# Feed-forward stages of a two-block transformer kernel: every other weight tile begins with the products with the weights' rest

## The reference

```python
def swiglu(h, w_gate, w_up, w_down):
    return (jax.nn.silu(h @ w_gate) * (h @ w_up)) @ w_down
```

```python
x = x + 0.5 * swiglu(rms_norm(x, ffn1_norm), ...)        # gu0, down0
x = x + concat(fourier, attention) @ w_out
x = x + 0.5 * swiglu(rms_norm(x, ffn2_norm), ...)        # gu1, down1
x = x + short_conv_mixer(...); x = x + mem_cross_attention(...)
x = x + swiglu_2(rms_norm_2(x, norm_ffn[0]), ...)        # gu2, down2
x = x + moba_attention(...);   x = x + mem_cross_attention(...)
x = x + swiglu_2(rms_norm_2(x, norm_ffn[1]), ...)        # gu3, down3
```

## Time and profile before

| what | value |
|---|---|
| median of 3 runs | 1240.12 us (1239.66 to 1240.19) |
| span of the profiled execution | 1237.7 us |
| mean granted clock of PE | 0.999 |
| PE busy | 1229.1 us (99%), 7432 matmuls |
| PEld busy | 1095.2 us (88%) |
| DVE busy | 928.1 us (75%) |
| ACT busy | 658.7 us (53%) |
| POOL busy | 31.1 us (3%) |
| DMA | 221.74 MB, mean 179 GB/s |
| L418, all (2716 in the feed-forward stages and those that share the helper) | 416.3 + 246.1 us |
| L1271 (DVE, rest of a weight tile) | x202, 2299 ns |
| L916 (ACT, rounding of a weight tile) | x202, 1911 ns |

### The profile page before, as it was taken

The page is one execution under the profiler, slowest core; times in us unless marked ns, Lnnn a source line. Parts: engine busy times, 40 slices in busy tenths (PEclk is TensorE's granted clock), DMA queues, the critical chain, the costliest instruction groups (busy, mean ns, idle before and its releaser), DMA issues.

```text
span 1237.7 us, 18082 instructions
## 1 busy us (share of the span) xinstructions
PE 1229.1 (99%) x7432; PEld 1095.2 (88%) x7432; DVE 928.1 (75%) x1292; ACT 658.7 (53%) x872; POOL 31.1 (3%) x23
## 2 busy tenths in 40 slices
PE   9999999999999999999999999999999999999998
PEld 8888889978888888888888888889998888888887
DVE  7887866878777858988568777669968657877744
ACT  6655544456555444546546555445555445555632
POOL 0000000000000000440000000000000000000000
PEclk9999999999999999999999999999999999999999
DMA  9565664235555663556346555644445533555560
GB/s 329 187 213 177 224 209 164 75 137 172 187 186 188 214 216 131 186 188 211 130 138 233 188 190 186 222 170 152 156 142 182 187 136 137 204 200 177 198 209 34
DMA packets 51426, 221.74 MB, mean 179 GB/s; under 512 B 4464, under 2 KB 5776, under 8 KB 30864
## 3 DMA queue, kind: packets, MB, share of 16 engines
q1 hardware_dynamic: 51056, 220.25, 51.7%
q10 hardware_dynamic: 288, 0.33, 0.1%
HBM read 219.52 MB, written 1.05 MB: 178 GB/s over the span
## 4 chain that ended last, share of the span: by engine, by line
PE 92%; DVE 5%; issue 1%; DMA 1%; ACT 0%; SPq 0%; DVEq 0%; ACTq 0%
PE bank L418 48%; PE bank L462 21%; PE bank L422 7%; PE bank L449 5%; PE bank L507 2%; DVE wt L1271 2%; PE bank L761 2%; PE bank L789 2%; PE bank L484 1%; PE bank L510 1%; PE bank L489 1%; DMA raw<-weights 1%; PE bank L777 0%; PE bank L544 0%; DVE xn L1280 0%
## 5 line engine op out<-in xcount | busy, mean ns | idle before, releaser
L1271 DVE TENSOR_TENSOR wt<-raw,wt 128x2048 fp32r<-128x2048 f32 x202 | 464.1, 2299 | 67.8 <-ACT wt L916 67.4
L916 ACT ACTIVATE wt<-raw 128x2048 fp32r<-128x2048 f32 x202 | 386.0, 1911 | 119.7 <-PE bank L422 89.8
L418 PE MATMUL bank<-xn,wt 128*128 128x512 f32 x1712 | 416.3, 393 | 1.4 <-DVE scratch L1376 0.7
L418 PEld LDWEIGHTS bank<-xn,wt 128*128 128x128 f32 x1712 | 313.0, 188 | 63.0 <-DVE xn L1280 1.1
L418 PE MATMUL bank<-h,wt 128*128 128x512 f32 x1004 | 246.1, 392 | 0.0
L462 PEld LDWEIGHTS bank<-xn,wt 128*128 128x128 f32 x1824 | 234.3, 191 | 9.7 <-DVE wt L1271 0.8
L462 PE MATMUL bank<-xn,wt 128*128 128x256 f32 x1824 | 238.2, 283 | 0.2 <-DVE wt L1271 0.2
L418 PEld LDWEIGHTS bank<-h,wt 128*128 128x128 f32 x1004 | 182.5, 188 | 34.1 <-issue 0.4
L1376 DVE TENSOR_TENSOR scratch<-bank,rest 128x512 f32<-128x512 f32 x98 | 67.6, 690 | 86.9 <-ACT rest L928 86.8
L999 ACT ACTIVATE h<-scratch 128x256 fp32r<-128x256 f32 x88 | 36.8, 418 | 158.7 <-DVE scratch L1416 158.7
L928 ACT ACTIVATE rest<-bank 128x512 f32<-128x512 f32 x114 | 67.6, 593 | 65.9 <-PE bank L462 64.4
(11 more groups left out here) (227 smaller groups left out, 972.3 us busy)
## 6 DMA issues: line engine op xcount, KB each, us to landing
raw<-weights SPq DMA_DIRECT2D x158, 1024.0 KB, 4.9
raw<-weights SPq DMA_DIRECT2D x88, 512.0 KB, 4.9
raw<-weights SPq DMA_DIRECT2D x8, 256.0 KB, 4.5
k_t<-mem_t SPq DMA_DIRECT2D x2, 1024.0 KB, 8.1
raw<-weights SPq DMA_DIRECT2D x8, 128.0 KB, 4.1
out_t<-work SPq DMA_DIRECT2D x4, 256.0 KB, 2.3
x<-x_t SPq DMA_DIRECT2D x3, 256.0 KB, 5.3
v_s<-fourier SPq DMA_DIRECT2D x2, 256.0 KB, 5.3
```

The lines of the kernel that those rows point to most:

```text
L418: return pe.matmul(out, hi, a.rearrange("p a s -> p (a s)"), start=first, stop=False, skip_group_check=True)
L916: act.activation(wt[t % RING][:, 0], raw[t % RING][:], ACT.Copy).then_inc(weight_hi, 1)
L1271: dve.tensor_tensor(wt[t % RING][:, 1], raw[t % RING][:], wt[t % RING][:, 0].bitcast(F32), ALU.subtract).then_inc(weight_lo, 1)
```

## The change

A turned order for some tiles of the feed-forward stages: first the 16 products with the rest (waiting for `weight_lo` before the first), then the 16 with the rounded weights; in `square_tile` under `turned`, in `down` as `turned_run`. Turned are, in the gate/up stages, the odd tiles from 3 on (in gu0 from 15 on), and in each down stage the slots 1, 3, 6 and 8. The products are the same, their order within the tile is another. The first product of a turned gate/up tile opens the bank (`start`) with the upper half alone, and the products with the rounded weights write the lower half for the first time with `start=False`.

```diff
+                if turned:
+                    pe.wait_ge(weight_lo, t + 1)
+                    for k in range(*ks):
+                        for m in range(ms):
+                            pe.matmul(out[:, m, S:2 * S], w[:, 1, m * KB + k, :], a[:, k, 0, :], start=k == 0, stop=False,
+                                      skip_group_check=True)
+                    for k in range(*ks):
+                        if k in beside:
+                            beside[k]()
+                        for m in range(ms):
+                            mm = pe.matmul(out[:, m, :], w[:, 0, m * KB + k, :], a[:, k].rearrange("p a s -> p (a s)"), start=False,
+                                           stop=k == KB - 1, skip_group_check=True)
+                    mm.then_inc(tile_done, 1)
+                    return
...
+            def turned_tile(n, j):
+                return j % 2 == 1 and j >= (15 if n == 0 else 3)
+
...
+                def turned_run(i, rows, d):
+
+                    w = wt[(t0 + i) % RING]
+                    blocks = [(at + m, k, bank[:, 2 * PAIR[name, 2 * d + m // 2] + m % 2, :]) for at, k in rows for m in range(4)]
+                    pe.wait_ge(weight_lo, t0 + i + 1)
+                    for at, k, out in blocks:
+                        with_rest(out, w[:, 1, at, :], h[:, k], False)
+                    for at, k, out in blocks:
+                        mm = with_hi(out, w[:, 0, at, :], h[:, k], False)
+                    return mm
...
-                    if i < FF // 4:
+                    if i in (1, 3):
+                        mm = turned_run(i, rows_at(0, range(4 * i, 4 * i + 4)), 0)
+                    elif i < FF // 4:
                         mm = run(i, rows_at(0, range(4 * i, 4 * i + 4)), 0, range(4), True)
...
+                    elif i in (6, 8):
+                        mm = turned_run(i, rows_at(0, range(4 * i - FF, 4 * i - FF + 4)), 1)
```

More of the change, by code:

```diff
@@ L422, in with_rest, with square_tile @@
                 return pe.matmul(out[:, S:2 * S], lo, a[:, 0, :], start=False, stop=last, skip_group_check=True)
-            def square_tile(t, out, a, ready=None, beside={}, lows=None, ks=(0, KB), ms=2, cuts=(), narrow=False, late=None):
+            def square_tile(t, out, a, ready=None, beside={}, lows=None, ks=(0, KB), ms=2, cuts=(), narrow=False, late=None, turned=False):
                 w = wt[t % RING]
+                if turned:
[12 more added lines that the diff above has]
+                    return
                 for k0, k1 in zip((ks[0], *cuts), (*cuts, ks[1])):
@@ L601, in gate_up @@
                                 cuts=((2, 4, 6) if j == 0 else (4,)) if in_parts else (4, 6) if j == 0 else (),
-                                late=KP * OPERAND[name] if j == 0 and n else None)
+                                    late=KP * OPERAND[name] if j == 0 and n else None, turned=turned_tile(n, j))
             def down(n_ffn, norm_name, beside={}):
```

## The result

| what | before | changed |
|---|---|---|
| median | 1239.73 us (1239.60 to 1240.19, 5 runs) | 1245.18 us (1245.12 to 1245.38, 5 runs) |
| ratio | | 1.0045, 95% interval 1.0033 to 1.0056 |
| span of the profiled execution | 1237.7 us | 1243.6 us |
| mean granted clock | 0.999 | 0.998 |

The changed kernel is 5.45 us slower. The forecast said slower, by 3.5 us, with a range from 1241.8 to 1245.3, which is 1.7 to 5.2 us above the median of 1240.12 that it stood on. The direction and the five places were right; the size was 2 us short and lies above that range. This is half again as much as forecast, so a term of the sum is missing or too small.

The account below looks back on a forecast made before the run. PE's instruction stream was taken as the bound. Profiled 1237.7 - 1.0 (switches) + 4.5 (late rests) = 1241.2 us; on the median, 1240.12 + 3.5 = 1243.7 us, range 1241.8 to 1245.3.

Parts of the forecast that it names:

- the five places: Tile 5 of gu1, gu2, gu3 and slot 1 of down0, down1: PE waits for late rests, 4.53 us in sum.
- PE's stream is the time, and a wait is lost whole: Whole run: PE is busy 99%, only 1.1 us of waits from 137 us on, so any new wait lengthens it equally.
- The delay is given back: Rival: a DVE that has caught up removes PE's later 1.1 us of waits on DVE or ACT, 1242.6 us; chance 0.11.
- Switches, 0.020 us for each turned tile: At 50 turned tiles, one pair of size switches saved each: 1.0 us gained, bounds 0 and 1.5.
- The switch saves nothing: Rival: turned tiles gain nothing from saved switches and the five waits stay, 1244.7 us; chance 0.13.
- the other side: Rival: a pair of switches is worth more than 0.02 us at every turned tile; at 0.11, 1239.1 us; chance 0.06.
- Which tiles are late: Of 50 turned tiles, 45 have at least 1.09 us to spare; five get DVE's rest 0.12 to 1.90 us late.
- Lateness + 0.15: Cost of a late rest: lateness plus 0.05 us to hear of it and 0.10 to get going; down1 2.05.
- Why they are late: Slot 1 of down0, down1: half tile 21 brings PE early, its quarter pieces queue ahead of L1271; 1.52, 1.90 late.
- The clock: Rival: PE's clock falls in the two long waits of down0 and down1, 1248.7 us; chance 0.06.
- The price of a fall: A fall behind a down wait costs 2.5 us, taken from the start-up's L798 products, which ran slow for 5.0 us.
- by it the two waits would cost about 5 us more: Down0 and down1 slot 1: by the skill's section, PE's waits can lower the clock, about 5 us for both.

Follow-up runs that it names:

- the next run: The changed kernel with 6 products of ones with ones in both waits, ahead of slot 1 of down0 and of down1: 1243.89 us.

## Why the prediction was right and where it was wrong

- **PE's stream is the time, and a wait is lost whole:** right. What was lost at down0 is still there 1100 us later; the rival "The delay is given back" falls. In the trace with the longer wait the whole addition stays to the end as well.
- **Switches, 0.020 us for each turned tile:** right, term and sign. Pairs take 0.02 less, and 45 of them measured 0.83 us against 0.9. That interval just touches no gain; the traces, in which every pair starts 0.02 us further ahead than the one before, decide it. The rival "The switch saves nothing" falls, and so does the other side.
- **Which tiles are late:** all five, and no sixth, with the lateness read from L1271's end against the tile's start. Tile 5 of gu1 to gu3 cost 0.34 to 0.39 each against 0.27 to 0.33, down0's slot 1 1.65 against 1.57. "Lateness + 0.15" was 0.02 to 0.12 too low at these places and at down1's slot 1 without the clock's part (2.10 against 2.05). The two parts of the 0.15 were also off, in opposite directions: the products start 0.15 us after L1303's end, where the earlier trace rows had 0.05, and the stretch behind the wait takes 0.07 to 0.08 us more than 1.91, not 0.10.
- **Why they are late (DVE's queue behind the half tile):** right; moving one step on DVE removed both waits and 5.2 us.
- **The clock:** here it failed. The step is "by the rows seen, nothing; no row decides for this length", after which the sum took the fall at nothing, and its chance was put at 0.06. What the runs showed in its place: one fall behind one of the two waits, worth 3.65 - 2.10 = 1.55 us at down1, or 3.15 - 1.65 = 1.5 us at down0 in the run with the wait of down1 filled (read at the start of slot 3; the expectation of the next run has 2.99). The longest wait that was weighed was 0.69 us; the new ones are more than twice as long, and silence of the trace was taken for an answer.
- **The price of a fall** was also wrong, in the other direction: 2.5 us by the start-up's slow stretch, which lasted 5 us. The one behind down1's wait lasted from 423.99 to 427.41, and half of that, 1.7 us, is the most that it could cost. Two falls were priced together, as if both or none came; every trace seen has one fall behind a wait, or none.
- **How near the repaired sum comes.** With one fall the forecast's own terms give 1243.7 + 1.55 = 1245.25, against 1245.18 measured. Part of this agreement is luck, since the forecast stood on 1240.12 and the kernel before measured 1239.73 beside the changed one: as a difference it is 5.1 against 5.45 us. The two profiled spans, 5.9 us apart, leave 0.8 us open, which the table above places: 0.26 in the start-up, 0.3 for waits a little dearer than forecast, 0.25 of the switches' gain that didn't come. The medians show less than half of it. Without the clock's part the difference is 4.00 us with both waits filled, against 3.5.
- **The rule that was weighed.** The section of the Trainium skill that was weighed (TensorE: Matmul & The Clock Gate, "HAM oscillation — how this bites in real kernels") pointed the right way: the trace agrees with it that waits of PE between groups of products can bring the clock down, here in the windows at 0.50 to 0.75. But the waits in that section's own case are longer than the two here, so "by it the two waits would cost about 5 us more" went beyond what it says.

The trace before did hold a sign, outside the rows used: at the end of the run, where PE has stopped. First its last row in the timeline, then the window over the end:

```profile
1232.03 0.38 PE L563 MATMUL bank<-con,col_x 128*128 128x128 f32 x2
1229.00:1237.00 8.00, 3.41 (x30) 3.17 (x29) 3.59 (x10) 2.21 (x6) 0.00 (x0) 0.86 0.35 131
```

PE's last product ends at 1232.41, and the mean clock of the window is 0.86: it is 1.00 up to 1234, 0.87 in the next microsecond and 0.50 from 1235 on. So the clock fell 2.3 us after PE stopped. That is no proof for a wait of 1.9 us, but it is nearer to it than 0.69. The page's slices of 31 us print a 9 over this fall as over a full clock.

What stays open is what makes the clock fall behind a given wait in one execution and not in the next. The four traces with a fall behind a wait (of 1.56, 1.88, 1.90 and 1.90 us) say this much: it came 0.4 to 0.7 us after PE had resumed, not in the wait. The five runs of the changed kernel all lie within 0.3 us, so each seems to have had one fall, though only one was profiled in detail.

## What to carry to other kernels

Before an engine's order is turned so that it asks for an operand earlier, lay the end of the operand's producer beside the new first use, for every instance and not for the steady state: 45 tiles had over a microsecond to spare here, and five decided the sign. Where the bound is PE, count a new wait of one to two microseconds with the clock behind it, some 1.5 us more, as a case with a real chance. A fall of some microseconds doesn't show in the page's slices; ask for the granted clock in narrow windows. And the same two tiles made PE wait for nothing once the producer's queue, not the consumer's, was reordered.

## What the runs showed of the hardware

- Behind a wait of PE of 1.56 us its clock fell to 1.2 GHz in one trace (down0, with down1's wait filled) and not in another (the changed kernel); behind 1.9 us it fell in all three traces that have such a wait at down1, and by the times in six or seven of the nine runs with that wait alone; behind 2.90 us it did not in one trace. A fall cost 1.5 to 1.6 us.
- Giving PE useless products to do in both waits (some 1.4 us of work in each) made the run 1.3 us shorter, with the data no earlier.
- A pair of switches between 512-column and 256-column products costs 0.02 us: each turned tile that saves one brings the later ones forward by that. Rests behind rests (32 in 3.84 us, 0.120 each) cost nothing extra across a tile's start, and rounded behind rounded (32 in 7.28, against 32 x 0.2264 + 0.03) next to nothing.
